# Scaling attention probabilities on GpSimd ahead of the transposes, in place of spread reciprocals behind the product with the values

## Chip, cores, metric

One core of a Trainium2 chip (trn2). The metric is the device time of one execution in microseconds (us), the median of several runs. The engines are TensorE (PE; its weight loads PEld), VectorE (DVE), ScalarE (ACT), GpSimd (POOL) and SyncE (SP). Each works through its own queue in order; they meet only at semaphores.

## The reference, cut to what matters

Two layers of a hybrid backbone over 512 latent tokens and 256 context tokens, width 1024, all in float32. Each layer is a SwiGLU block, a token mixing, and a second SwiGLU block. The change touches the softmax attention inside the mixing:

```
def attend(q, k, v, scale):
    s = jnp.einsum('bqhd,bkhd->bhqk', q, k).astype(jnp.float32) * scale
    p = jax.nn.softmax(s, axis=-1).astype(v.dtype)
    return jnp.einsum('bhqk,bkhd->bqhd', p, v)
...
ya_x = blocked_attention(qa_x, jnp.concatenate([ka_c, ka_x], axis=1), jnp.concatenate([va_c, va_x], axis=1), MLA_SCALE)
yb_x = neighborhood_attention(qb_x, kb_x, vb_x, kb_c, vb_c, na_rpb, rows)
ya_c = attend(qa_c, ka_c, va_c, MLA_SCALE)     # layer 0 only, as yb_c
```

Eight heads of latent attention (query and key width 96, value width 64) and four heads of neighbourhood attention (width 64, with a position bias on the latent keys). Latent queries see 512 latent and 256 context keys; context queries, which only layer 0 needs, see the 256 context keys.

## The kernel before

Every float32 product is made of three: an operand is split into a high part (a rounded copy, by ACT) and a low part (the difference, by DVE or GpSimd), and TensorE adds high x high, high x low and low x high.

In each layer the attention is one loop over **chunks**: 128 queries of one head against all their keys. A pair of heads has 12 chunks in layer 0 (per head four of latent queries with 768 keys, two of context queries with 256) and 8 in layer 1 (four per head). There are six such pairs, four latent and two neighbourhood: 72 and 48 chunks. Every engine runs through a list of steps s written out by hand, several chunks in flight:

- TensorE (`attention_pe`, from L1471), step s: the scores of chunk s into one of two PSUM pairs (L1487 to L1489, behind the exp of chunk s - 2); the transposes of chunk s - 2 from `prob` into the single PSUM buffer `pmid` (L1503, behind its exp and behind the low half of chunk s - 3); half of the products with V of the pair of chunks that began at s - 4 (L1522 to L1524). Ahead of the first half of a pair it waits for the reciprocals and makes, for each of the two chunks, a product of the reciprocals, broadcast, with the identity (L1515). This spreads 1/sum, which lies one per partition (query), over the free axis, where the queries are once the values have been multiplied in.
- DVE (`attention_dve`, from L1598), step s: for latent queries of neighbourhood heads the scores plus bias into `prob` (L1612, L1614); the negated maximum of chunk s (L1617); the reciprocal of the sum of chunk s - 1 (L1623); for even s the multiplication of the copied result of a finished pair, `y_f`, by the spread reciprocals (L1630, behind ACT's copy); the low half of the transposed chunk s - 2 (L1638, `pt_lo`).
- ACT (`attention_act`, from L1533), step s: the high half of chunk s - 2 from `pmid` (L1556, `pt_hi`), for even s the copy of a finished pair from PSUM to `y_f` (L1563), then exp of chunk s with the sum of its row (L1570), and at the first chunk of a head the high parts of the next head's q and k (L1531). `prob` has three slots, `pmid` one, `pt_hi` and `pt_lo` four.
- GpSimd (`attention_pool`, from L1578): at the first chunk of a head both low parts of the next head (L1586; ahead of the first neighbourhood pair those of V too, 1536 columns wide), and at step 7 of a pair of heads the low part of a finished block of y (L1595; three blocks in the fifth pair). Else it is idle in the loop.

`a_exp`, `a_rsum`, `a_ptl`, `a_pv`, `a_out`, `a_copied` are the semaphores of exp, reciprocal, low half, product with V, finished y, copied y.

Of the kernel before, what the change touches and what calls it, by code (L numbers as in the profile page):

```python
# [29 lines left out]
P = 128  # L30
# [135 lines left out]
def program(nc, x, c, ctx_in, c_ctx, w_mod, b_mod, w_gate, w_up, w_down, w_in, g_cq, w_q_up, g_ckv, w_kv_up,  # L166
            g_mla_q, g_mla_k, g_na_q, g_na_k, na_rpb, w_pool, pool_scale, w_out,
            k_ident, k_perm, k_cos, k_sin, k_invcnt, out, na_bias):
    with ExitStack() as ctx:
        def sem(name):  # L170
            return ctx.enter_context(nc.semaphore(name))
# [5 lines left out]
        def sb(name, shape, dt, at=None, off=0):  # L177
# [127 lines left out]
        a_hi, a_lo, v_hi_done = sem("a_hi"), sem("a_lo"), sem("v_hi_done")  # L305
        a_s, a_max, a_exp, a_rsum, a_copied, a_t, a_pth, a_ptl, a_pv, a_out, a_bias = (
            sem(f"a_{k}") for k in ("s", "max", "exp", "rsum", "copied", "t", "pth", "ptl", "pv", "out", "bias"))
        a_latent_t, a_latent_hi, a_latent_lo = (sem(f"a_latent_{k}") for k in ("t", "hi", "lo"))
# [1162 lines left out]
        def attention_pe(eng, l):  # L1471
# [4 lines left out]
            for s in range(n + 4):  # L1476
# [14 lines left out]
                if 2 <= s < n + 2:  # L1491
                    c = s - 2
                    keys = chunk_info(l, c)[4]
                    eng.wait_ge(a_exp, c0 + c + 1)
                    for part, (a, b) in enumerate(PARTS):
# [9 lines left out]
                if s >= 4:  # L1505
# [3 lines left out]
                    if part == 0:  # L1509
                        eng.wait_ge(a_ptl, c0 + 2 * b + 2)  # L1510
                        wait_if(eng, a_out, c0 // 2 + b - 1)
                        eng.wait_ge(a_rsum, c0 + 2 * b + 2)
                        for h in range(2):
                            at = (b % 2) * 512 + (2 + h) * P
                            eng.matmul(psum2[:, at:at + P], stat[:, (2 * b + h) % STATS, 2:3].broadcast_to([P, P]),  # L1515
                                       ident[:, :], start=True, stop=True)
                    vh, vl = (v_hi, v_lo) if kind == "mla" else (vn_hi, vn_lo)
# [15 lines left out]
        def attention_act(eng, l):  # L1533
# [8 lines left out]
            for s in range(n + 5):  # L1542
# [15 lines left out]
                if s >= 6 and s % 2 == 0:  # L1558
# [4 lines left out]
                    eng.activation(y_f[r, i if kind == "mla" else 4 + i, q0:q0 + 2 * P], psum2[r, bank:bank + 2 * P],  # L1563
                                   ACT.Copy).then_inc(a_copied, 1)
                if s < n:
# [12 lines left out]
        def attention_pool(eng, l):  # L1578

            n, w = n_chunks(l), y_cols(l)[-1][1]  # L1580

            def split(g):
                first, operands = splits(g)
                for m, (src, hi, lo) in enumerate(operands):
                    eng.wait_ge(a_hi, ATT_SPLITS * l + first + m + 1)
                    eng.tensor_tensor(lo, src, hi.bitcast(F32), ALU.subtract).then_inc(a_lo, 1)  # L1586

            split(0)
            for s in range(n):
                g, new = att_group(l, s)  # L1590
                if new and g + 1 < GROUPS:
                    split(g + 1)
                for k in y_split_at(l, s):
# [4 lines left out]
        def attention_dve(eng, l):  # L1598

            c0, n = ATT_C0[l], n_chunks(l)  # L1600
            for s in range(n + 5):
# [16 lines left out]
                if 1 <= s <= n:  # L1618
                    c = s - 1
                    eng.wait_ge(a_exp, c0 + c + 1)  # L1620
                    if c >= STATS:
                        eng.wait_ge(a_pv, c0 // 2 + (c - STATS) // 2 + 1)
                    eng.reciprocal(stat[:, c % STATS, 2:3], stat[:, c % STATS, 1:2]).then_inc(a_rsum, 1)  # L1623
                if s >= 6 and s % 2 == 0:
                    b = (s - 6) // 2
                    kind, i, j, q0, _ = chunk_info(l, 2 * b)
                    r, bank = slice(j * 64, j * 64 + 64), (b % 2) * 512
                    y = y_f[r, i if kind == "mla" else 4 + i, q0:q0 + 2 * P]
                    eng.wait_ge(a_copied, c0 // 2 + b + 1)
                    eng.tensor_tensor(y, y, psum2[r, bank + 2 * P:bank + 4 * P], ALU.mult).then_inc(a_out, 1)  # L1630
                if 2 <= s < n + 2:
# [256 lines left out]
```

## Time and profile before

| | us |
|---|---|
| median of 3 runs | 3387.88 (3383.86 to 3390.73) |
| the profiled execution | 3380.54 |
| its span | 3379.0 |
| TensorE busy | 3233.9 (96%), 18746 matmuls |
| DVE busy | 1709.8 (51%) |
| ACT busy | 928.8 (27%) |
| GpSimd busy | 212.5 (6%) |

The profile is one execution. Its page gives busy time by engine, the span in 40 slices, the chain that ended last and the costliest groups of instructions; the trace behind it can be asked for the busy time of a stretch, for who waited for whom, and for the instructions in order of time. Matmuls overlap in their records (a product starts before the one ahead has ended), so distances between starts say more than durations. A few matmul records are missing. The loops lie at about 1004 to 1218 us (layer 0) and 2786 to 2947 us (layer 1).

### The profile page before, as it was taken

Reading aid. Unit: us, or ns where it says so; the run is one execution under the profiler, and the core shown is the slowest. Engines: PE = TensorE matmul, PEld = TensorE weight load, DVE = VectorE, ACT = ScalarE, POOL = GpSimd, SP = SyncE. Lnnn points to the kernel's source line nnn. Section 1 sums busy time; section 2 is a strip of 40 time slices with the busy share of each in tenths; the row PEclk is TensorE's granted clock in tenths of the full one; section 3 lists DMA queues with packets and bytes.
Section 4 is the critical chain, followed back from the end, with each engine's and each line's share of the span. In section 5 each row is a group of like instructions: output and inputs, shape, how many; then the busy total and the mean of one; then the engine's idle time right before and its main releaser. Section 6 shows DMA issues by size and latency. Waiting matters only on the chain. (4 is left out here: it accounts for less than half of the span.)

```text
span 3379.0 us, 48465 instructions
## 1 busy us (share of the span) xinstructions
PE 3233.9 (96%) x18746; PEld 2818.9 (83%) x18746; DVE 1709.8 (51%) x2923; ACT 928.8 (27%) x1399; POOL 212.5 (6%) x181
## 2 busy tenths in 40 slices
PE   6999999989999998999999899999989999999999
PEld 6888888878888877888888788888878889878887
DVE  2665366354356755652664665263354257743333
ACT  1211122122136642211222221112222237633221
POOL 0500000030002200000000000000020003200000
PEclk7899999999999998999999899999999999999999
DMA  4633233221100012332332233242112100123333
GB/s 156 143 121 117 80 122 107 76 62 48 37 12 1 24 38 75 122 120 64 123 121 73 81 121 107 65 124 82 56 53 56 31 7 12 37 80 99 95 94 93
DMA packets 418467, 264.73 MB, mean 78 GB/s; under 512 B 21604, under 2 KB 409224, under 8 KB 418344
## 3 DMA queue, kind: packets, MB, share of 16 engines
q1 hardware_dynamic: 413512, 254.16, 25.4%
q0 software_dynamic: 2752, 4.66, 0.8%
q10 hardware_dynamic: 2080, 4.19, 0.4%
q8 instruction: 86, 1.41, 0.2%
q14 instruction: 37, 0.30, 0.0%
HBM read 257.15 MB, written 6.68 MB: 78 GB/s over the span
## 5 line engine op out<-in xcount | busy, mean ns | idle before, releaser
L361 PE MATMUL pair<-h_hi,w_hi 128*128 128x512 f32 x3136 | 1103.7, 352 | 47.4 <-DVE h_lo L477 21.5
L362 PE MATMUL pair<-h_lo,w_hi 128*128 128x512 f32 x3136 | 1030.3, 347 | 0.0
L365 PE MATMUL pair<-h_hi,w_lo 128*128 128x512 f32 x3136 | 869.0, 348 | 0.0
L361 PEld LDWEIGHTS pair<-h_hi,w_hi 128*128 128x128 f32 x3136 | 598.0, 191 | 190.3 <-issue 49.6
L362 PEld LDWEIGHTS pair<-h_lo,w_hi 128*128 128x128 f32 x3136 | 598.7, 191 | 77.4
L335 DVE TENSOR_TENSOR w_lo<-w_raw,w_hi 128x1024 fp32r<-128x1024 f32 (+2 forms) x310 | 399.6, 1290 | 459.2 <-ACT w_hi L328 450.8
L328 ACT ACTIVATE w_hi<-w_raw 128x1024 fp32r<-128x1024 f32 (+2 forms) x310 | 337.5, 1090 | 735.1 <-PE pair L365 691.3
L365 PEld LDWEIGHTS pair<-h_hi,w_lo 128*128 128x128 f32 x3136 | 504.8, 192 | 16.8
L361 PE MATMUL pair<-s_hi,w_hi 128*128 128x512 f32 x1232 | 426.6, 346 | 0.0
L362 PE MATMUL pair<-s_lo,w_hi 128*128 128x512 f32 x1232 | 400.5, 344 | 0.0
L600 DVE SCALAR_TENSOR_TENSOR mod_acc<-mod_raw,cs,mod_acc 128x256 f32<-128x256 f32 x896 | 365.1, 478 | 0.0
L365 PE MATMUL pair<-s_hi,w_lo 128*128 128x512 f32 x1232 | 339.5, 345 | 0.0
L745 DVE SCALAR_TENSOR_TENSOR xT<-pair,mv,xT 128x512 f32 (+3 forms) x136 | 81.8, 636 | 490.6 <-PE pair L365 490.1
L361 PEld LDWEIGHTS pair<-s_hi,w_hi 128*128 128x128 f32 x1232 | 231.3, 188 | 54.3
L362 PEld LDWEIGHTS pair<-s_lo,w_hi 128*128 128x128 f32 x1232 | 231.4, 188 | 30.0
L721 ACT ACTIVATE s_hi<-sf 128x768 f32 (+3 forms) x88 | 69.8, 793 | 634.6 <-DVE sf L768 634.6
L365 PEld LDWEIGHTS pair<-s_hi,w_lo 128*128 128x128 f32 x1232 | 196.2, 190 | 6.8
L718 ACT ACTIVATE sg<-pair 128x768 f32<-128x768 f32 (+1 forms) x88 | 66.8, 759 | 426.3 <-PE pair L365 426.3
L768 DVE TENSOR_TENSOR sf<-pair,sg 128x768 f32<-128x768 f32 (+1 forms) x88 | 78.4, 890 | 173.1 <-PE pair L365 173.0
L771 DVE TENSOR_TENSOR s_lo<-sf,s_hi 128x768 f32 (+3 forms) x88 | 78.5, 892 | 92.0 <-ACT s_hi L721 92.0
L1638 DVE TENSOR_TENSOR pt_lo<-pmid,pt_hi 128x512 fp32r<-128x512 f32 (+1 forms) x216 | 107.5, 534 | 24.5 <-ACT pt_hi L1556 23.1
L1556 ACT ACTIVATE pt_hi<-pmid 128x512 fp32r<-128x512 f32 (+1 forms) x216 | 92.6, 475 | 93.8 <-PE pmid L1503 93.6
(192 smaller groups left out, 3466.3 us busy)
## 6 DMA issues: line engine op xcount, KB each, us to landing
mod_raw<-in_w_mod SPq DMA_DIRECT2D x64, 1024.0 KB, 5.0
w_raw<-in_w_ffn_gate SPq DMA_DIRECT2D x88, 512.0 KB, 3.8
w_raw<-in_w_ffn_up SPq DMA_DIRECT2D x88, 512.0 KB, 3.8
w_raw<-in_w_ffn_down SPq DMA_DIRECT2D x64, 704.0 KB, 4.6
w_raw<-in_w_in SPq DMA_DIRECT2D x34, 512.0 KB, 3.9
w_raw<-in_w_out SPq DMA_DIRECT2D x12, 512.0 KB, 4.0
w_raw<-in_w_q_up SPq DMA_DIRECT2D x16, 288.0 KB, 2.9
mod_first<-in_w_mod ACTq DMA_DIRECT2D x2, 2048.0 KB, 12.6
```

The source lines that it names most:

```text
L328: eng.activation(w_hi[:, t.odd, 0:w], raw[:, t.odd, 0:w], ACT.Copy).then_inc(w_hi_done, 1)
L335: eng.tensor_tensor(w_lo[:, t.odd, 0:w], raw[:, t.odd, 0:w], w_hi[:, t.odd, 0:w].bitcast(F32), ALU.subtract).then_inc(w_lo_done, 1)
L361: eng.matmul(dst, wh, rh, start=first, stop=False)
L362: eng.matmul(dst, wh, rl, start=False, stop=False)
L365: last = eng.matmul(dst, wl, rh, start=False, stop=end)
L600: eng.scalar_tensor_tensor(mod_acc[:, j, :], mod_raw[:, k, :], cs[:, k, j:j + 1], mod_acc[:, j, :], ALU.mult, ALU.add).then_inc(mod_step, 1)
L721: eng.activation(s_hi[:, bass.ds(i, 1), 0:w].rearrange("p a t -> p (a t)"), sf[:, 0:w], ACT.Copy).then_inc(s_hi_done, 1)
L745: last = eng.scalar_tensor_tensor(xT[:, bass.ds(d, 1), a:b].rearrange("p a t -> p (a t)"), pair[o.odd][:, a:b], mv[:, 2, bass.ds(d, 1), p] ...
L768: eng.tensor_tensor(sf[:, 0:w], pair[(o + 1).odd][:, 0:w], sg[:, 0:w], ALU.mult).then_inc(acc_free[(o + 1).odd], 1)
L771: eng.tensor_tensor(s_lo[:, bass.ds(i, 1), 0:w].rearrange("p a t -> p (a t)"), sf[:, 0:w], s_hi[:, bass.ds(i, 1), 0:w].bitcast(F32).rearra ...
L1556: eng.activation(pt_hi[:, a // P:b // P, c % 4, :], pmid[:, a:b].rearrange("p (k q) -> p k q", q=P), ACT.Copy).then_inc(a_latent_hi if a = ...
L1638: eng.tensor_tensor(pt_lo[:, a // P:b // P, c % 4, :], pmid[:, a:b].rearrange("p (k q) -> p k q", q=P), pt_hi[:, a // P:b // P, c % 4, :]. ...
```

## The change

The reciprocals are applied earlier and by another engine. GpSimd waits for the reciprocal of chunk s and multiplies `prob` of that chunk in place by it, one value per partition. The transposes wait for this (`a_norm`) where they waited for exp. The spread reciprocals on TensorE (L1515) and the multiplication of `y_f` on DVE (L1630) go; ACT's copy is the finished y. GpSimd's low parts, which were made together at the first chunk of a head, are dealt out: one operand behind the multiplication of each of the first chunks.

```
@@ attention_pe
-                    eng.wait_ge(a_exp, c0 + c + 1)
+                    eng.wait_ge(a_norm, c0 + c + 1)
...
                         eng.wait_ge(a_ptl, c0 + 2 * b + 2)
                         wait_if(eng, a_out, c0 // 2 + b - 1)
-                        eng.wait_ge(a_rsum, c0 + 2 * b + 2)
-                        for h in range(2):
-                            at = (b % 2) * 512 + (2 + h) * P
-                            eng.matmul(psum2[:, at:at + P], stat[:, (2 * b + h) % STATS, 2:3].broadcast_to([P, P]),
-                                       ident[:, :], start=True, stop=True)
@@ attention_act
-                                   ACT.Copy).then_inc(a_copied, 1)
+                                   ACT.Copy).then_inc(a_out, 1)
@@ attention_pool
-            split(0)
+            for m in range(2):
+                split(0, m)
+            at = 0
             for s in range(n):
                 g, new = att_group(l, s)
-                if new and g + 1 < GROUPS:
-                    split(g + 1)
+                at = 0 if new else at + 1
+                a = chunk_info(l, s)[4][0][0]
+                eng.wait_ge(a_rsum, c0 + s + 1)
+                eng.tensor_scalar(prob[:, s % 3, a:TOK], prob[:, s % 3, a:TOK], stat[:, s % STATS, 2:3], None,
+                                  ALU.mult).then_inc(a_norm, 1)
+                if g + 1 < GROUPS and at < len(splits(g + 1)[1]):
+                    split(g + 1, at)
@@ attention_dve
                     if c >= STATS:
-                        eng.wait_ge(a_pv, c0 // 2 + (c - STATS) // 2 + 1)
+                        eng.wait_ge(a_norm, c0 + c - STATS + 1)
                     eng.reciprocal(stat[:, c % STATS, 2:3], stat[:, c % STATS, 1:2]).then_inc(a_rsum, 1)
-                if s >= 6 and s % 2 == 0:
-                    b = (s - 6) // 2
-                    kind, i, j, q0, _ = chunk_info(l, 2 * b)
-                    r, bank = slice(j * 64, j * 64 + 64), (b % 2) * 512
-                    y = y_f[r, i if kind == "mla" else 4 + i, q0:q0 + 2 * P]
-                    eng.wait_ge(a_copied, c0 // 2 + b + 1)
-                    eng.tensor_tensor(y, y, psum2[r, bank + 2 * P:bank + 4 * P], ALU.mult).then_inc(a_out, 1)
```

## Rows read from the trace of the kernel before

**Rows 1.** The page: span, and busy us (share) xinstructions by engine.
```profile
span 3379.0 us, 48465 instructions
...
PE 3233.9 (96%) x18746; PEld 2818.9 (83%) x18746; DVE 1709.8 (51%) x2923; ACT 928.8 (27%) x1399; POOL 212.5 (6%) x181
```

**Rows 2.** Stretches, both loops: length, busy by engine, granted clock, DMA share, GB/s.
```profile
1008.00:1218.00 210.00, 186.83 (x1335) 168.78 (x1333) 145.03 (x332) 138.28 (x325) 48.74 (x26) 0.98 0.05 15
2788.00:2948.00 160.00, 152.96 (x1100) 140.17 (x1099) 123.74 (x252) 113.59 (x244) 45.02 (x26) 0.99 0.06 19
```

**Rows 3.** TensorE's waits in the same two stretches: us, times, longest.
```profile
PE pmid L1503 <- DVE pt_lo L1638: 20.1, 32, 1.2
...
PE pmid L1503 <- DVE pt_lo L1638: 2.8, 4, 1.0
```

**Rows 4.** Timeline, latent attention of layer 1: start, length, engine, line [idle before].
```profile
2804.38 0.82 PE L1503 MATMUL pmid<-ident,prob 128*128 128x128 f32 x6
...
2805.41 0.36 PE L1522 MATMUL psum<-pt_hi,v_hi 128*128 128x256 f32 x1
...
2805.46 0.15 DVE L1623 RECIPROCAL stat<-stat 128x1 f32<-128x1 f32 x1
...
2807.61 0.82 PE L1503 MATMUL pmid<-ident,prob 128*128 128x128 f32 x6
2807.81 0.96 DVE L1617 TENSOR_REDUCE stat<-pair 128x1 f32<-128x768 f32 x1 [0.22 <-PE pair L1489]
2808.19 0.36 PE L1522 MATMUL psum<-pt_hi,v_hi 128*128 128x256 f32 x1
...
2813.82 0.96 DVE L1617 TENSOR_REDUCE stat<-pair 128x1 f32<-128x768 f32 x1 [0.23 <-PE pair L1489]
```

**Rows 5.** Timeline, DVE, layer 0: maximum at the start of two sixes.
```profile
1022.28 0.96 DVE L1617 TENSOR_REDUCE stat<-pair 128x1 f32<-128x768 f32 x1 [0.69 <-PE pair L1489]
...
1121.50 0.96 DVE L1617 TENSOR_REDUCE stat<-pair 128x1 f32<-128x768 f32 x1 [0.63 <-PE pair L1489]
```

**Rows 6.** Timeline, layer 0: three turns of the ring, the second with L1630.
```profile
1046.73 0.85 PE L1503 MATMUL pmid<-ident,prob 128*128 128x128 f32 x6 [0.65 <-DVE pt_lo L1638]
1048.93 0.84 PE L1503 MATMUL pmid<-ident,prob 128*128 128x128 f32 x6 [0.64 <-DVE pt_lo L1638]
1052.26 0.85 PE L1503 MATMUL pmid<-ident,prob 128*128 128x128 f32 x6 [0.60 <-DVE pt_lo L1638]
...
1050.96 0.42 DVE L1630 TENSOR_TENSOR y_f<-y_f,psum 64x256 f32<-64x256 f32 x1 [1.45 <-ACT y_f L1563]
1051.42 1.02 DVE L1638 TENSOR_TENSOR pt_lo<-pmid,pt_hi 128x512 fp32r<-128x512 f32 x2
```

**Rows 7.** One line of the code, GpSimd's copies: shortest/median/longest ns.
```profile
L1380 POOL COPY k_f<-kr_f x16: 816/822/1353, 864.8 to 2652.9; 32x768 f32<-32x768 f32 x16
```

**Rows 8.** Groups by shape, GpSimd: busy us, mean ns, idle before.
```profile
L1586 POOL TENSOR_TENSOR qs_lo<-na_f,qs_hi 128x768 fp32r<-128x768 f32 x4 | 7.4, 1845 | 36.8 <-ACT qs_hi L1531 36.8
...
L1586 POOL TENSOR_TENSOR vn_lo<-vn_f,vn_hi 128x1536 fp32r<-128x1536 f32 x2 | 7.0, 3486 | 0.0
L1595 POOL TENSOR_TENSOR h_lo<-y_f,h_hi 128x512 fp32r<-128x512 f32 x5 | 6.5, 1291 | 43.1 <-ACT h_hi L1464 43.1
```

**Rows 9.** Timeline, neighbourhood attention of layer 1: a pair of chunks; transposes and reciprocal.
```profile
2892.33 0.95 DVE L1617 TENSOR_REDUCE stat<-prob 128x1 f32<-128x768 f32 x1
...
2894.73 0.87 PE L1503 MATMUL pmid<-ident,prob 128*128 128x128 f32 x6
...
2896.76 0.15 DVE L1623 RECIPROCAL stat<-stat 128x1 f32<-128x1 f32 x1
...
2899.01 0.95 DVE L1617 TENSOR_REDUCE stat<-prob 128x1 f32<-128x768 f32 x1
```

**Rows 10.** Timeline, DVE, layer 0: first bias of two neighbourhood heads, three sixes apart.
```profile
1138.84 0.69 DVE L1612 TENSOR_TENSOR prob<-pair,na_tt 128x512 f32<-128x512 f32 x1 [0.81 <-PE pair L1489]
...
1195.58 0.69 DVE L1612 TENSOR_TENSOR prob<-pair,na_tt 128x512 f32<-128x512 f32 x1 [0.82 <-PE pair L1489]
```

More of the change, by code:

```diff
@@ L305, in program @@
         a_hi, a_lo, v_hi_done = sem("a_hi"), sem("a_lo"), sem("v_hi_done")
-        a_s, a_max, a_exp, a_rsum, a_copied, a_t, a_pth, a_ptl, a_pv, a_out, a_bias = (
-            sem(f"a_{k}") for k in ("s", "max", "exp", "rsum", "copied", "t", "pth", "ptl", "pv", "out", "bias"))
+        a_s, a_max, a_exp, a_rsum, a_norm, a_t, a_pth, a_ptl, a_pv, a_out, a_bias = (
+            sem(f"a_{k}") for k in ("s", "max", "exp", "rsum", "norm", "t", "pth", "ptl", "pv", "out", "bias"))
         a_latent_t, a_latent_hi, a_latent_lo = (sem(f"a_latent_{k}") for k in ("t", "hi", "lo"))
@@ L1578, in attention_pool, with split @@
         def attention_pool(eng, l):
-            n, w = n_chunks(l), y_cols(l)[-1][1]
-            def split(g):
+            c0, n, w = ATT_C0[l], n_chunks(l), y_cols(l)[-1][1]
+            def split(g, m):
                 first, operands = splits(g)
-                for m, (src, hi, lo) in enumerate(operands):
-                    eng.wait_ge(a_hi, ATT_SPLITS * l + first + m + 1)
-                    eng.tensor_tensor(lo, src, hi.bitcast(F32), ALU.subtract).then_inc(a_lo, 1)
-            split(0)
+                src, hi, lo = operands[m]
+                eng.wait_ge(a_hi, ATT_SPLITS * l + first + m + 1)
+                eng.tensor_tensor(lo, src, hi.bitcast(F32), ALU.subtract).then_inc(a_lo, 1)
+            for m in range(2):
+                split(0, m)
+            at = 0
             for s in range(n):
                 g, new = att_group(l, s)
-                if new and g + 1 < GROUPS:
-                    split(g + 1)
+                at = 0 if new else at + 1
[5 more added lines that the diff above has]
+                    split(g + 1, at)
                 for k in y_split_at(l, s):
```

## Prediction

> **What bounds the kernel now.** I began with the page: TensorE is busy for 96% of the span, so time goes where TensorE's work is shortened or where it waits [rows 1]. The change touches only the two attention loops, so the second view is the table of stretches: the loop of layer 0 takes 210 us with 186.8 us of TensorE, that of layer 1 160 us with 153.0, both at 0.98 to 0.99 of the full clock [rows 2]. Everything else is untouched, and what follows a loop starts when the loop ends. The third view, TensorE's waits, tells the loops apart: in layer 0 its transposes (L1503) wait 20.1 us in 32 pieces for the low halves of DVE (L1638), in layer 1 2.8 us [rows 3]. The fourth is the timeline.
>
> In layer 1's latent attention TensorE is the bound. Two chunks take 6.01 us, from maximum to maximum. From the transposes to the products with V it takes 1.03 us in the chunk with the spread reciprocals (L1515) and 0.58 us in the other [rows 4]: L1515 costs 0.45 us a pair. A chunk of 768 keys without it is (6.01 - 0.45)/2 = 2.78 us, of which I give 0.68 to the transposes and 1.05 each to scores and to values (both stream 2304 columns). A context chunk (256 keys) takes a third: 0.93.
>
> In layer 0 each head has four full chunks and two context chunks, a "six". TensorE's work on a six is 4 x 2.78 + 2 x 0.93 + 3 x 0.45 = 14.3 us, yet the six sixes from 1022.28 to 1121.50 take 16.54 us each [rows 5]. The rest is a ring through the single buffer pmid: transposes, high half on ACT, low half on DVE, next transposes. Undisturbed it turns in 2.20 us (1046.73 to 1048.93), but where the multiplication by the reciprocals (L1630) stands ahead of L1638 on DVE and waits for ACT's copy, in 3.33 (1048.93 to 1052.26) [rows 6].
>
> **What the change takes away.** L1515: 60 pairs x 0.45 = 27 us of TensorE, worth that only where TensorE doesn't wait for something else. L1630: 0.42 us of DVE per pair, and its wait ahead of L1638.
>
> **What it adds.** 120 GpSimd multiplications, 96 of 768 columns and 24 of 256,, and a place for them in the path: maximum, exp, reciprocal, GpSimd, transposes. The scaled chunk c is wanted at step c + 2. Its reciprocal stands on DVE behind the maximum of chunk c + 1. Call E(c) the end of the issue of the scores of chunk c. Then the reciprocal of c begins at E(c+1) + 1.08 (2804.38 to 2805.46) and lasts 0.15 [rows 4]; with 0.08 to reach GpSimd, a multiplication of length m and 0.05 to reach TensorE, the transposes of c can begin at E(c+1) + 1.36 + m. They are due at E(c+2), 2.78 later. So m up to 1.42 is hidden where GpSimd has nothing else to do; beyond it every us costs half a us a chunk, because the delay returns every second step.
>
> The price m is in no row. From below: GpSimd's one-input copy of 768 columns, 0.82 us [rows 7]; from above: its two-input subtraction of 768 columns, 1.84 us [rows 8]. The multiplication has one wide input and one value per partition, so it is nearest to the copy: I take 0.95 (0.35 for 256 columns), an estimate: 0.82 plus an allowance of about 0.13 for fetching the value. The Trainium skill, GPSIMD Engine Reference, section 4.1, speaks against putting elementwise work on GpSimd (about half VectorE's speed with two inputs) but calls one input roughly line-rate. The two kinds of row, 1.84 and 0.82, agree with it. By its section 3.1 (1.03 cycles an element at 1.2 GHz for a port-bound loop) the body would be an estimated 0.66 us, under my lower bound; the sum would be some 20 us better than mine.
>
> **What is queued on GpSimd.** It also makes the low halves of the next head's q and k: before, both at once; now each behind the multiplication of the first and second chunk. A multiplication plus a subtraction is 0.95 + 1.80 = 2.75 us a step (start to start), just inside 2.78: in layer 1 this is hidden for m = 0.95, and for nothing larger. Three things aren't hidden. (a) In layer 0 the steps of a six are shorter (E to E 2.33, 2.33, 2.08, 1.38, 2.08, 2.78), so the queue costs time. (b) The low half of V for the neighbourhood heads takes 3.49 us [rows 8]; it now starts behind the third chunk of the last latent head. (c) The low halves of y (1.84 us in layer 0, 1.29 in layer 1 [rows 8]) fall between two multiplications, three in a row once per layer.
>
> **The sum, m = 0.95.**
> Layer 1, latent (32 chunks, TensorE-bound): 16 x 0.45 = 7.2 gained. V's low half begins at E(31) + 2.25 and ends at E(31) + 5.7, where the scores of chunk 32 were due at E(31) + 1.73: 4.0 lost.
> Layer 1, neighbourhood (16 chunks): now 6.68 a pair, 3.34 a chunk. The bias is added on DVE first, so the reciprocal begins at E + 2.03 (2894.73 to 2896.76) [rows 9]; two steps take 2.03 + 0.15 + 0.08 + 0.95 + 0.05 + 2.78 = 6.04, or 3.02 a chunk: 16 x 0.32 = 5.1 gained. Three low halves of y in a row (3.9 us against a slack of 2.1): 1.8 lost. At the end the last ring turns without L1630 and L1515: 1.0 gained.
> Together 7.2 - 4.0 + 5.1 - 1.8 + 1.0 = 7.5 gained.
> Layer 0, latent (8 sixes): with the ring at 2.20 and no queue on GpSimd a six would be 14.04. With it: the first multiplication ends at E(1) + 2.26, q's half at + 4.10, the second multiplication at + 5.05, k's half at + 6.89, the third at + 7.84; its transposes begin at + 7.89, the fourth's a ring later (+ 10.1), and with 2.78 + 2.33 to the next E(1) the six is 15.2 us. With a low half of y it is 17.0, with V's too 19.3. Four sixes of 15.2 gain 1.34 each, 5.4; two of 17.0 lose 0.9; the last loses 2.0 (from 17.3); the first gains 0.5. Together 3.0.
> Layer 0, neighbourhood (4 sixes): the three from 1138.84 to 1195.58 take 18.9 each [rows 10]. By the same steps with the longer DVE part a six becomes 15.8, and 19.3 with three low halves of y: 7.7 gained over the four. The loop's end: 1.0. Together 3.0 + 7.7 + 1.0 = 11.7.
> All: 7.5 + 11.7 = 19.2 us gained. The profiled execution (3380.5, span 3379.0) would come to 3361.3; the median of the runs shown, 3387.9, lies 7.3 above it, so I name 3387.9 - 19.2 = 3368.7, rounded to 3369.
>
> **The rivals.**
> A, slower: the multiplication costs GpSimd what a two-input one does, 1.84 us [rows 8]. In layer 1 the transposes of the first two chunks of a head then begin at E(1) + 3.2 and + 6.8, the next two at + 10.4 and + 13.2; four chunks take 13.2 us, not 12.0, 9 us over eight heads; V and y cost 5 more, and the neighbourhood chunks at 3.5 instead of 3.34 another 5: 19 lost. In layer 0 a six goes from 16.5 to 17.7 and to 19.5 with y, 16 for the latent heads, and 9 for the rest: 25 lost. 44 lost in all, 3432. For it: every elementwise row of GpSimd in the loops has this price. Against: all of them have two wide inputs. Between 0.95 and 1.84 the sum moves by 63/0.89 = 71 us per us, so it decides from m = 1.22 us on.
> B, no change: m between 1.12 and 1.31 puts gain and loss within 7 us, 3388. The removed L1515 and L1630 are then paid back by the queue on GpSimd.
> C, a larger gain: m at the copy's 0.82 and the first scaled chunks catching up within a six. Then the 27 us of L1515 come nearly whole and some of layer 0's 20.1 us of waiting: about 35 gained, 3353. Against: the queue's arithmetic above.
>
> **How the numbers follow.** Forecast 0.48; C 0.08; B 0.19; A 0.25. The forecast's own range is 3354 to 3380. The range has to take in B and the near part of A (m up to about 1.5: 3369 + 71 x 0.55 = 3408): 3352 to 3410, about 0.8. A measurement of this kernel can tell some 0.2% (6.8 us) from no change. Faster by more: forecast and C, 0.56; within: B, 0.19; slower: A, 0.25.
>
> **What would show it.** GpSimd's multiplications at 0.95 us for 768 columns, and two chunks of layer 1's latent heads at 5.56 us instead of 6.01, confirm the first two steps. TensorE's waits for pmid in layer 0 should now name GpSimd's prob where they named DVE's pt_lo, mostly in the second and third chunk of a head. One wait of about 4 us should stand before the scores of layer 1's first neighbourhood chunk, ended by GpSimd. Layer 1's neighbourhood chunks should come every 3.0 us. If m is above 1.4 even the quiet chunks of layer 1 wait, and the forecast is wrong in sign; if the waits on GpSimd are missing although m is near 0.95, the queue was overpriced and C is nearer.

## Result, and the profile after

The changed kernel takes 3478.41 us (median of 4 runs, 3475.90 to 3479.58), the kernel before 3386.66 (4 runs). The ratio is 1.0277, 95% interval 1.0264 to 1.0289: slower by 92 us. I had named 3369, with a range of 3352 to 3410 and 0.56 on faster. The time is outside the range, and the sign is wrong. In the experiments below one of the four executions of removed ran at a granted clock of 0.53 and took 6371.53 us; its ratio and interval leave it out.

| | before | after |
|---|---|---|
| median, us | 3386.66 | 3478.41 |
| profiled execution, its span | 3380.54, 3379.0 | 3475.90, 3474.1 |
| loop of layer 0, first scores to first output product | 216.4 | 277.5 |
| the same in layer 1 | 162.8 | 201.2 |
| a six (four full and two context chunks) of a latent head, layer 0, no low half of y behind it | 16.2 to 16.8 | 20.3 to 21.0 |
| a six with a low half of y behind it | 16.2 and 16.5 | 23.3 |
| four chunks of a latent head, layer 1 | 12.1 | 14.4 |

The two loops hold all of it: 61.1 + 38.4 = 99.5 us, against 95.1 in the span; the rest of the kernel came to 4.4 us less in this pair of executions.

The page of the changed kernel, its first lines and two of its costliest groups (answering [rows 1]):

```profile
span 3474.1 us, 48043 instructions
...
PE 3248.8 (94%) x18506; PEld 2825.0 (81%) x18506; DVE 1690.5 (49%) x2863; ACT 926.7 (27%) x1399; POOL 443.9 (13%) x301
...
PEclk6899999999988889999999999999999999899999
...
L1591 POOL TENSOR_SCALAR prob<-prob,stat 128x768 f32<-128x768 f32 x96 | 211.1, 2202 | 80.9 <-DVE stat L1625 80.9
...
L1591 POOL TENSOR_SCALAR prob<-prob,stat 128x256 f32<-128x256 f32 x24 | 22.2, 923 | 67.8 <-DVE stat L1625 67.8
```

The disputed price stands in the last two lines. GpSimd's multiplication of 768 columns takes 2.20 us, not 0.95; that of 256 columns 0.92, not 0.35. This is more than the upper bound I had set, 1.84 us. The trace of the kernel before had dearer GpSimd rows of about this width, outside the loops: a two-tensor multiplication of 64x776 at 2.23 us (L1370) and an addition of 128x791 at 2.58 (L1361). The prediction left them out. TensorE has 240 matmuls fewer and is still busy for 15 us more. The line PEclk (granted clock in tenths of full speed, 40 slices) has four slices of 8 where layer 0's loop runs.

The stretches that hold the two loops now (columns as in [rows 2]: length, busy PE, PEld, DVE, ACT, POOL with their counts, granted clock, DMA share, GB/s):

```profile
1008.00:1281.00 273.00, 201.74 (x1188) 180.31 (x1188) 133.68 (x297) 139.48 (x329) 175.32 (x98) 0.83 0.04 11
...
2846.00:3044.00 198.00, 157.29 (x996) 138.34 (x996) 115.28 (x227) 113.75 (x245) 149.81 (x74) 0.91 0.05 15
```

GpSimd went from 48.7 to 175.3 us in the first and from 45.0 to 149.8 in the second. The granted clock fell from 0.98 to 0.83 and from 0.99 to 0.91.

TensorE's waits in the same two stretches (what and where, who ended it: us, times, longest), answering [rows 3]:

```profile
PE pmid L1503 <- POOL prob L1591: 67.0, 40, 5.7
...
PE pmid L1503 <- POOL prob L1591: 27.5, 32, 2.7
PE pair L1487 <- POOL vn_lo L1581: 5.4, 1, 5.4
```

Where layer 0's transposes waited 20.1 us for DVE's low halves, they wait 67.0 for GpSimd's scaled probabilities; in layer 1 it was 2.8 and is 27.5. The single wait of 5.4 us is the low half of V, the one I had put at 4.0.

The timeline of one latent head in layer 1 shows how a step now runs (start, length, engine, line, [idle before and who ended it]), answering [rows 4]:

```profile
2863.77 2.20 POOL L1591 TENSOR_SCALAR prob<-prob,stat 128x768 f32<-128x768 f32 x1 [1.39 <-DVE stat L1625]
...
2865.94 1.83 POOL L1581 TENSOR_TENSOR qs_lo<-q_f,qs_hi 96x768 fp32r<-96x768 f32 x1
...
2866.03 0.87 PE L1503 MATMUL pmid<-ident,prob 128*128 128x128 f32 x6 [0.59 <-POOL prob L1591]
...
2867.76 2.20 POOL L1591 TENSOR_SCALAR prob<-prob,stat 128x768 f32<-128x768 f32 x1
...
2869.93 1.84 POOL L1581 TENSOR_TENSOR ks_lo<-k_f,ks_hi 96x768 fp32r<-96x768 f32 x1
...
2870.01 0.87 PE L1503 MATMUL pmid<-ident,prob 128*128 128x128 f32 x6 [0.99 <-POOL prob L1591]
...
2871.74 2.20 POOL L1591 TENSOR_SCALAR prob<-prob,stat 128x768 f32<-128x768 f32 x1
...
2874.00 0.88 PE L1503 MATMUL pmid<-ident,prob 128*128 128x128 f32 x6 [0.86 <-POOL prob L1591]
...
2878.16 2.20 POOL L1591 TENSOR_SCALAR prob<-prob,stat 128x768 f32<-128x768 f32 x1 [1.65 <-DVE stat L1625]
```

From 2863.77 to 2871.74 GpSimd has no gap: 2.20 + 1.80 = 4.0 us a step, where TensorE wants 2.78. The transposes begin 0.05 to 0.07 us behind each multiplication. 14.39 us lie between the first line and the last, the same place one head on. That is the queue of the prediction, with the other price. Put 2.20 into its chain, with E(1) again the end of the issue of the scores of chunk 1, and the transposes begin at E(1) + 3.56, + 7.56, + 11.56 and + 14.34, so a head takes 14.35 us; measured 14.4.

Layer 0 has a second effect, which the sum had not at all. Two waits on GpSimd in a row (transposes, timeline), and then four stretches of 3 us around them:

```profile
1077.30 0.88 PE L1503 MATMUL pmid<-ident,prob 128*128 128x128 f32 x6 [1.70 <-POOL prob L1591]
...
1083.04 1.54 PE L1503 MATMUL pmid<-ident,prob 128*128 128x128 f32 x6 [4.15 <-POOL prob L1591]
```

```profile
1079.00:1082.00 3.00, 0.00 (x0) 0.00 (x0) 1.39 (x4) 1.09 (x3) 3.00 (x3) 1.00 0.01 3
1082.00:1085.00 3.00, 1.96 (x9) 1.97 (x10) 0.12 (x1) 0.75 (x2) 3.00 (x2) 0.51 0.00 0
1085.00:1088.00 3.00, 3.00 (x16) 3.00 (x15) 1.40 (x4) 0.83 (x4) 0.39 (x2) 0.50 0.00 0
1088.00:1091.00 3.00, 3.00 (x21) 2.87 (x20) 1.17 (x3) 1.32 (x4) 0.69 (x1) 0.85 0.00 0
```

TensorE waits 4.15 us for a multiplication that stands behind a low half of y. Then the granted clock is 0.50 (the lower level, 1.2 GHz) for some six microseconds of dense work: the six transposes take 1.54 us in place of 0.88. Sixes without y are touched too. In each of them the transposes wait about 1.1, 1.7 and 2.4 us for GpSimd in a row, and behind the third the transposes took 0.96 to 1.54 us; the sixes of 20.3 us ran at a mean clock of 0.92, those of 21.0 at 0.84. In the kernel before, the sixes ran at 1.00.

### The profile page after: what moved, and what is told of

Read it like the earlier page. It is cut to its first block and busy times, and to the rows that moved or that the text cites. A ratio compares the mean times of both kernels' runs of the same rounds, so it can differ in the third digit from the quotient of the medians.

```text
span 3474.1 us, 48043 instructions
## 1 busy us (share of the span) xinstructions
PE 3248.8 (94%) x18506; PEld 2825.0 (81%) x18506; DVE 1690.5 (49%) x2863; ACT 926.7 (27%) x1399; POOL 443.9 (13%) x301
## 3 DMA queue, kind: packets, MB, share of 16 engines
q1 hardware_dynamic: 413512, 254.16, 24.5%
## 5 line engine op out<-in xcount | busy, mean ns | idle before, releaser
L365 PEld LDWEIGHTS pair<-h_hi,w_lo 128*128 128x128 f32 x3136 | 502.6, 191 | 16.7
L1591 POOL TENSOR_SCALAR prob<-prob,stat 128x768 f32<-128x768 f32 (+1 forms) x120 | 233.2, 1946 | 148.7 <-DVE stat L1625 148.7
L1503 PE MATMUL pmid<-ident,prob 128*128 128x128 f32 x624 | 112.0, 321 | 96.6 <-POOL prob L1591 94.5
L1503 PEld LDWEIGHTS pmid<-ident,prob 128*128 128x128 f32 x624 | 81.8, 163 | 115.7 <-POOL prob L1591 112.4
## 6 DMA issues: line engine op xcount, KB each, us to landing
mod_first<-in_w_mod ACTq DMA_DIRECT2D x2, 2048.0 KB, 12.4
```

Source lines behind the costliest of these rows:

```text
L365: last = eng.matmul(dst, wl, rh, start=False, stop=end)
L1503: last = eng.transpose(pmid[:, k * P:(k + 1) * P], prob[:, c % 3, k * P:(k + 1) * P], ident[:, :])
L1591: eng.tensor_scalar(prob[:, s % 3, a:TOK], prob[:, s % 3, a:TOK], stat[:, s % STATS, 2:3], None, ALU.mult).then_inc(a_norm, 1)
```

## Experiments

Two theories stood after this, which may both be true in part. **P (price):** my chain is right and only m was wrong; a GpSimd multiplication of 0.9 us would give the forecast time. **C (clock and the rest):** there are costs that the chain lacks, so that even at 0.9 us the forecast isn't reached. A third question was why m is 2.20: the form of the instruction, its operand of one value per partition, or the place beside DVE. The length of a six is the distance between the first maxima of two heads, as in [rows 5]; four chunks of layer 1 likewise. A "plain" six has no low half of y or V behind it.

### m_256: the price brought down to 0.92 us

```
-                eng.tensor_scalar(prob[:, s % 3, a:TOK], prob[:, s % 3, a:TOK], stat[:, s % STATS, 2:3], None,
+                eng.tensor_scalar(prob[:, s % 3, SEQ:TOK], prob[:, s % 3, SEQ:TOK], stat[:, s % STATS, 2:3], None,
```

> The changed kernel, but GpSimd multiplies only the last 256 columns of each chunk (the 512 latent columns stay unscaled, so that part of the computation is left out). The trace of the changed kernel has 0.92 us for a multiplication of this width and 2.20 us for 768. Theory P (the price of the multiplication was the wrong term, the rest of the sum holds): at about 0.92 us the forecast's sum applies, some 19 us below the kernel before, 3364 to 3376. Rival Q (the added link and the low halves queued behind it cost by themselves, whatever the multiplication takes): no gain or a loss, 3385 or more.

Measured: 3386.10 us against 3384.65, ratio 1.0001 (0.9991 to 1.0011). The multiplications took 922 ns. Every second latent head of layer 1 took 11.13 us for its four chunks, 5.56 a pair, which is the forecast's figure; the heads between took 11.4. A plain six took 15.07 (forecast 15.2). But a six with a low half of y took 19.2 (forecast 17.0), the fifth pair's with three of them 22.9 (19.3), a plain neighbourhood six 17.65 (15.8). The whole time is the one expected by the rival, 3385 or more, and not P's 3364 to 3376. Place by place, P is right in the plain latent sixes and heads and misses 17 us (3386 against 3369) elsewhere. The price explains 92 of the 109 us between forecast and result, and not all.

### removed: only what the change takes away

The kernel before without L1512 to L1516 and without L1624 to L1630.

> The kernel before without the spread reciprocals on TensorE (L1515) and without the multiplication of y (L1630), nothing in their place, so the probabilities stay undivided: the removals alone, GpSimd as before. Theory P: the ring of layer 0 turns in 2.20 us throughout and a six takes about 14.0 us instead of 16.5, layer 1's latent pairs 5.56 us instead of 6.01; together 35 to 45 us gained, about 3345. If the removed products lay beside other work, less than 10 us.

Measured: 3346.53 against 3384.65, 0.9876 (0.9856 to 0.9896), 38 us less. A six took 14.05 us, where the chain with the ring at 2.20 says 14.04; four latent chunks of layer 1 took 11.13 and 11.4 in turn. The gain of taking these two things away was there, and as large as expected (35 to 45). In the neighbourhood heads of layer 1 a chunk came every 3.12 us, not 2.95 to 3.02. A plain neighbourhood six of layer 0 took 16.7, where the forecast had 15.8. The timeline of DVE alone, in layer 1, says why:

```profile
2866.23 0.95 DVE L1612 TENSOR_REDUCE stat<-prob 128x1 f32<-128x768 f32 x1
2867.10 0.15 DVE L1618 RECIPROCAL stat<-stat 128x1 f32<-128x1 f32 x1
2867.17 1.00 DVE L1626 TENSOR_TENSOR pt_lo<-pmid,pt_hi 128x512 fp32r<-128x512 f32 x2
2868.30 0.69 DVE L1607 TENSOR_TENSOR prob<-pair,na_tt 128x512 f32<-128x512 f32 x1
2868.91 0.41 DVE L1609 COPY prob<-pair 128x256 f32<-128x256 f32 x1
2869.36 0.95 DVE L1612 TENSOR_REDUCE stat<-prob 128x1 f32<-128x768 f32 x1
```

No idle time in brackets: from maximum to maximum (2866.23 to 2869.36) DVE works without a gap for 3.13 us. The bound is DVE, at 3.12 a chunk, and no order of GpSimd's work gets below it.

### norm_dve: the same multiplication on DVE

GpSimd's low halves stand together at the first chunk of a head again, as in the kernel before. The main lines of the edit:

```
-                eng.tensor_scalar(prob[...], ..., ALU.mult).then_inc(a_norm, 1)      # GpSimd, L1591
...
                     eng.reciprocal(stat[:, c % STATS, 2:3], stat[:, c % STATS, 1:2]).then_inc(a_rsum, 1)
+                    a = chunk_info(l, c)[4][0][0]
+                    eng.wait_ge(a_rsum, c0 + c + 1)
+                    eng.tensor_scalar(prob[:, c % 3, a:TOK], prob[:, c % 3, a:TOK], stat[:, c % STATS, 2:3], None,
+                                      ALU.mult).then_inc(a_norm, 1)
```

> The same scaling ahead of the transposes, but by DVE, right behind its reciprocal, and GpSimd's low halves at the first chunk of a head as before. No row shows this form on DVE; its other forms of 768 columns take 0.70 (memset) to 0.96 us (maximum), so 0.5 to 0.9 is likely. Theory P: TensorE's wait on GpSimd is gone; layer 1's latent heads stay at 5.56 us a pair, the neighbourhood heads, which DVE bounds, get slower by 0.2 to 0.4 us a chunk; within 12 us of the kernel before on either side, 3375 to 3400, and far below the changed kernel. Rival Q (scaling ahead of the transposes is what costs, on whichever engine): near the changed kernel, 3440 or more.

Measured: 3408.60 against 3384.65, 1.0071 (1.0054 to 1.0087), outside the expected 3375 to 3400. DVE's multiplication, all 120 of it (shortest/median/longest ns), then two of them beside GpSimd:

```profile
L1621 DVE TENSOR_SCALAR prob<-prob,stat x120: 352/620/3424, 1008.9 to 2965.5; 128x768 f32<-128x768 f32 x96, 128x256 f32<-128x256 f32 x24
```

```profile
2867.16 1.85 POOL L1581 TENSOR_TENSOR qs_lo<-q_f,qs_hi 96x768 fp32r<-96x768 f32 x1 [8.46 <-ACT qs_hi L1526]
...
2867.40 2.02 DVE L1621 TENSOR_SCALAR prob<-prob,stat 128x768 f32<-128x768 f32 x1
...
2871.32 0.62 DVE L1621 TENSOR_SCALAR prob<-prob,stat 128x768 f32<-128x768 f32 x1
```

Alone it takes 0.62 us, a third of GpSimd's 2.20. Where GpSimd is in a low half (2867.16 to 2869.01) the same instruction takes 2.02 and ends 0.41 after GpSimd's, as if it had stood for most of that time. On DVE the step is cheaper, but it is held up when it meets GpSimd, and the rest of DVE's queue with it. In layer 0's loop TensorE waits 26.8 us for DVE's low halves and 8.7 for its multiplication.

### forms: four forms in one kernel

The changed kernel, with another form in each of three pairs of heads per layer.

```
+                if pair_n == 1:
+                    eng.tensor_scalar(dst, dst, 0.5, None, ALU.mult).then_inc(a_norm, 1)
+                elif pair_n == 2:
+                    eng.tensor_tensor(dst, dst, stat[:, s % STATS, 2:3].broadcast_to([P, TOK - a]), ALU.mult).then_inc(a_norm, 1)
+                elif pair_n == 3:
+                    eng.tensor_copy(dst, dst).then_inc(a_norm, 1)
```

> The changed kernel with another form of GpSimd's instruction in three of the six pairs of heads: second pair a constant (0.5) in place of the value per partition, third pair a product of two tensors with the reciprocal broadcast along the row, fourth pair a copy in place (these pairs are not divided by their sum, except the third). For the price of 768 columns. If fetching the value per partition is what is dear: constant near the copy's 0.82 us. If the form itself is: constant 2.2 us too, copy 0.82, two tensors 1.84 or more. The pairs with the copy should take 5.56 us per two chunks, those with 1.84 us about 6.6 in layer 1.

Measured in one execution, GpSimd's groups by shape (busy us, mean ns, idle before):

```profile
L1599 POOL TENSOR_SCALAR prob<-prob,stat 128x768 f32<-128x768 f32 x48 | 105.7, 2206 | 67.7 <-DVE stat L1632 67.7
...
L1593 POOL TENSOR_SCALAR prob<-prob 128x768 f32<-128x768 f32 x16 | 34.0, 2127 | 7.0 <-DVE stat L1632 7.0
...
L1595 POOL TENSOR_TENSOR prob<-prob,stat 128x768 f32<-128x768 f32 x16 | 23.4, 1465 | 7.4 <-DVE stat L1632 7.4
...
L1597 POOL COPY prob<-prob 128x768 f32<-128x768 f32 x16 | 13.2, 827 | 15.6 <-DVE stat L1632 15.6
```

Same buffer, same columns, same place. The value per partition is not the reason: with a constant it is 2127 against 2206 ns. The place isn't either: a copy there takes 827, as in [rows 7]. It is the form: the tensor-with-scalar form is the dearest of the four on GpSimd, dearer than the subtraction of two full tensors (1845, [rows 8]), and the two-tensor form with the reciprocals spread by the access pattern does the same arithmetic in 1465. Why the form is so dear, no run shows. The whole took 3454.71 us. The first sixes of the pairs of layer 0 follow the form: 20.1 us with the constant, 16.6 with the spread reciprocals, 14.7 with the copy.

### low_dve: the full price, without the queue

The changed kernel; the low halves of q, k, V and y go from GpSimd to DVE, behind its own low half of the chunk. Only the multiplications stay on GpSimd.

> The changed kernel with the full multiplication on GpSimd (2.20 us for 768 columns) and nothing else there: all low halves, of q, k, V and y, are made by DVE. Tells the price of the link itself from that of the queue. By the chain, reciprocal at E + 1.08, plus 0.28, plus 2.20, every second step: 3.17 us a chunk in layer 1's latent heads, 12.7 us a head (changed kernel 14.4), a six about 16.5 (changed 20.3 to 23.3); in all 3400 to 3420, so still 15 to 35 us slower than before. If the queue of low halves were harmless: 3470 or more. If it were the whole cost: 3385 or less.

Measured: 3438.00 against 3384.10, 1.0154 (1.0137 to 1.0171). The expected range, 3400 to 3420, is missed. Taking the low halves off GpSimd gives back about 40 us (3478.4 - 3438.0) net of what DVE pays for them, and 54 are left with the link of 2.20 us and that work. Four chunks of layer 1 took 13.0 us (expected 12.7). The latent sixes took 17.5 to 20.4, mostly 18.7, well over the 16.5 expected. The granted clock goes with them: the six of 17.5 ran at 1.00, those of 18.6 to 19.0 at 0.91, that of 20.4 at 0.83. Even at 1.00 a six is 1.0 us over the chain; that part wasn't separated from DVE's longer list.

### m_256_y: low halves of y and V off GpSimd, m at 0.92

m_256, with the low halves of y and V on DVE, those of q and k left on GpSimd.

> m_256 again (GpSimd multiplies only the last 256 columns, the rest stays unscaled), but the low halves of y and of V, which queued on GpSimd between two multiplications, are made by DVE; those of q and k stay. In m_256 the plain sixes of layer 0 take 15.07 us (forecast 15.2) and the heads of layer 1 11.13, but the sixes with a low half of y 19.2 (forecast 17.0) and the head with that of V 18.9 us. Theory P with this correction: these all fall to the plain ones, 20 to 27 us gained on m_256, about 3362. If instead the scaling ahead of the transposes costs something spread over all chunks: less than 8 us gained.

Measured: 3379.06 against 3384.10, 0.9984 (0.9975 to 0.9994), 5 us less where 22 were expected, and 7 less than m_256. The four chunks with V's low half fell from 18.86 to 15.98 us, but the sixes with y stayed at 19.4. DVE and GpSimd met again:

```profile
1059.88 1.84 POOL L1581 TENSOR_TENSOR qs_lo<-q_f,qs_hi 96x768 fp32r<-96x768 f32 x1
...
1060.35 2.19 DVE L1649 TENSOR_TENSOR h_lo<-y_f,h_hi 128x768 fp32r<-128x768 f32 x1
```

DVE's subtraction of two SBUF tensors, 0.95 us where it is alone, takes 2.19 beside a GpSimd low half. The next maximum and reciprocal stand behind it on DVE, so GpSimd's next multiplication starts late, TensorE waits 2.22 us for it, and the six runs at a clock of 0.82, as in m_256. The wait moved from GpSimd's queue to DVE's and cost the same.

### m_256_fill: the same wait with the clock held up

m_256, with products of the identity with itself (their result is not used) written into a spare region of PSUM, ahead of the transposes that wait for a multiplication behind y.

```
+                    late = len(y_split_at(l, c - 1)) if c else 0
+                    if late and s < n:
+                        ...
+                        for h in range((12 if l == 0 else 6) * late):
+                            at = (b % 2) * 512 + 2 * P
+                            eng.matmul(psum2[:, at:at + P], ident[:, :], ident[:, :], start=True, stop=True)
```

> m_256 with idle products (identity x identity, 0.22 us each, 12 for each low half of y in layer 0, 6 in layer 1) put on TensorE ahead of the transposes that wait for GpSimd behind a low half of y. The wait stays as long; TensorE only doesn't stand still in it. In m_256 the granted clock falls to 0.50 for about 6 us behind such a wait of 2.87 us. Theory R (the fall of the clock is the part of those sixes that the forecast missed): the clock stays at 1.00 and the sixes with y fall from 19.2 to about 17.0 us, the forecast's value. Rival (the queue alone makes them 19.2): they stay at 19.2 or get longer.

Measured in the latent sixes with y: 16.85 us against 19.2 in m_256, and 17.0 in my prediction. First m_256, without the filling: one late group of transposes and the stretches from its wait on:

```profile
1067.27 1.54 PE L1503 MATMUL pmid<-ident,prob 128*128 128x128 f32 x6 [2.87 <-POOL prob L1591]
```

```profile
1065.00:1068.00 3.00, 0.73 (x4) 0.73 (x5) 0.90 (x4) 0.60 (x2) 3.00 (x3) 0.64 0.00 0
1068.00:1071.00 3.00, 3.00 (x16) 3.00 (x14) 1.02 (x2) 1.57 (x5) 0.12 (x1) 0.50 0.00 0
1071.00:1074.00 3.00, 3.00 (x19) 2.96 (x19) 1.52 (x4) 1.32 (x4) 0.92 (x1) 0.72 0.00 0
```

and with it:

```profile
1058.87 2.84 PE L1500 MATMUL psum<-ident 128*128 128x128 f32 x24
...
1061.91 0.88 PE L1510 MATMUL pmid<-ident,prob 128*128 128x128 f32 x6 [0.20 <-POOL prob L1598]
```

```profile
1059.00:1062.00 3.00, 2.80 (x26) 2.61 (x25) 1.42 (x4) 1.23 (x4) 3.00 (x4) 1.00 0.01 3
1062.00:1065.00 3.00, 3.00 (x26) 2.91 (x27) 1.45 (x4) 1.71 (x6) 0.91 (x2) 1.00 0.00 0
```

The same GpSimd queue, the same wait, filled with useless work: the clock stays at 1.00, the transposes take 0.88 instead of 1.54, and the six is 2.3 us shorter. This shows the clock term by itself, in this place. The whole kernel took 3390.24 (one execution), not less than m_256. The plain neighbourhood sixes went from 17.65 to 18.7 and 18.9, that with three low halves of y from 22.9 to 24.5, and in layer 1 the latent heads with y from 11.4 to 12.4: there the filling was longer than the wait it was to fill. So it shows the mechanism in the latent sixes and is no better kernel.

### shared: the two engines each scale a part

Two-tensor form on GpSimd for 512 columns, DVE's multiplication for the 256 context columns, of the latent heads. DVE also scales the chunks of context queries, which have only those columns, and makes y's and V's low halves; GpSimd scales the neighbourhood chunks of 768 columns alone.

> A complete kernel. The reciprocals still go ahead of the transposes, but as cheaply as the runs allow: for latent heads GpSimd multiplies the 512 latent columns, with the two-tensor form and the reciprocal broadcast (1.47 us for 768 columns and 0.61 for 256 in the run of forms, so about 1.04 for 512), DVE the 256 context columns (0.35 us) at the same time; neighbourhood chunks with 768 keys by GpSimd alone (1.47); the low halves of y and V on DVE. By the same chain: reciprocal at E + 1.08, 0.28, 1.04, so hidden in layer 1 (11.2 us a head), sixes about 15.3; 10 to 22 us faster than the kernel before, about 3368. If any link ahead of the transposes costs more than it gives back: 3385 or more.

Measured: 3415.76 against 3384.10, 1.0086 (1.0069 to 1.0103); expected about 3368. It was the furthest miss of the runs:

```profile
2862.59 1.23 DVE L1649 TENSOR_SCALAR prob<-prob,stat 128x256 f32<-128x256 f32 x1
...
2862.63 1.04 POOL L1608 TENSOR_TENSOR prob<-prob,stat 128x512 f32<-128x512 f32 x1 [0.26 <-DVE stat L1646]
```

Both wait for the same reciprocal, so in the latent chunks they start together, and DVE's part, 0.35 us alone, takes a median of 1.23: longer than GpSimd's own 1.04. The split didn't let the two parts run side by side. How much of the miss this explains wasn't separated: DVE also has the low halves of y and V here.

### tt_form: the change in its cheaper form

```
-                eng.tensor_scalar(prob[:, s % 3, a:TOK], prob[:, s % 3, a:TOK], stat[:, s % STATS, 2:3], None,
-                                  ALU.mult).then_inc(a_norm, 1)
+                eng.tensor_tensor(prob[:, s % 3, a:TOK], prob[:, s % 3, a:TOK],
+                                  stat[:, s % STATS, 2:3].broadcast_to([P, TOK - a]), ALU.mult).then_inc(a_norm, 1)
```

> The changed kernel with one thing different: GpSimd multiplies with the two-tensor form, the reciprocal broadcast along the row, which took 1.47 us for 768 columns and 0.61 for 256 in the run of forms (the changed kernel's form 2.20 and 0.92). A complete kernel. If the time follows the price m (m_256 3386 at 0.92, changed kernel 3478 at 2.20, 72 us per us): about 3425. If the price of 768 columns hardly matters beyond the link: near 3470.

Measured: 3416.42 against 3385.74, 1.009 (1.0075 to 1.0105); expected about 3425. One instruction's form, 2.20 to 1.465 us, is worth 62 us (3478.4 - 3416.4), two thirds of the loss. Latent heads of layer 1 come back to 12.1 us, as before the change. The chain says the same: a multiplication and a low half are 1.47 + 1.80 = 3.27 us a step, 0.49 over 2.78, twice in a head, on top of 11.13.

### all_dve: nothing on GpSimd in the loop

norm_dve, with the low halves on DVE as well.

> norm_dve (DVE multiplies) with the low halves of q, k, V and y made by DVE as well, so that GpSimd does nothing in the loops. In norm_dve DVE's multiplication of 768 columns took 0.62 us in the median and up to 3.42. If the long ones are DVE standing still while GpSimd reads and writes: here all take about 0.62 us, and DVE's two-input low halves of 768 columns 0.95; if they come from something else they stay. Total by DVE's load (0.88 + 0.13 + 0.62 + 0.95, and 1.9 for q and k once a head): about 3.1 us a chunk in layer 1, 3390 to 3410.

Measured in one execution:

```profile
L1621 DVE TENSOR_SCALAR prob<-prob,stat x120: 352/620/622, 1010.3 to 2982.7; 128x768 f32<-128x768 f32 x96, 128x256 f32<-128x256 f32 x24
```

The longest multiplication falls from 3424 to 622 ns when GpSimd is idle: the long ones in norm_dve were the meeting of the two engines, nothing else. The time, 3421.59, is above the expected 3390 to 3410. In layer 1 the latent heads are DVE's: it is busy for 59.8 of 62.0 us (2838 to 2900), at a clock of 1.00. In layer 0 this isn't so: over the sixes from 1041.7 to 1135.7, 18.8 us each, DVE is busy for 73.5 of 94.0 us, TensorE waits 13.6 us in ten pieces for DVE's low halves, and the granted clock is 0.82. So moving everything to DVE brings waits and a fallen clock too; no run says what each costs.

### y_last: from the other end

The kernel before, with L1624 to L1630 moved behind L1638 in DVE's list, and nothing else. The wait for ACT's copy then stands behind the low half that the ring needs.

> The kernel before with one thing moved: DVE's multiplication of y by the spread reciprocals (L1630) stands behind the low half of the transposed chunk (L1638) and no longer ahead of it. A complete kernel; nothing of the change is in it. In the run of removed both L1515 and L1630 were gone and a six took 14.05 us instead of 16.54. If the forecast's ring is right, of these 2.5 us 1.35 are L1515 (3 x 0.45) and the rest is L1630 standing in the way: a six of about 15.4 here, layer 1's latent heads unchanged at 12.1, in all 9 to 16 us faster than before, about 3372. If the move gains nothing: TensorE's queue, not the ring, bounds the sixes.

Measured: 3366.94 against 3385.74, 0.9949 (0.9934 to 0.9963): 19 us less than the kernel before (expected 9 to 16), 111 less than the changed one. Plain sixes took 15.2 us (expected 15.4). The transposes' waits in layer 0's loop (1008 to 1210), and the turn of the ring that follows the moved multiplication (here L1631 is the low half, L1640 the multiplication):

```profile
PE pmid L1503 <- DVE pt_lo L1631: 13.7, 14, 1.7
```

```profile
1045.80 0.42 DVE L1640 TENSOR_TENSOR y_f<-y_f,psum 64x256 f32<-64x256 f32 x1
...
1045.92 0.82 PE L1503 MATMUL pmid<-ident,prob 128*128 128x128 f32 x6
...
1048.14 0.85 PE L1503 MATMUL pmid<-ident,prob 128*128 128x128 f32 x6 [0.69 <-DVE pt_lo L1631]
```

The turn is 2.22 us (1045.92 to 1048.14), where with L1630 in front it was 3.33 [rows 6], and the 20.1 us of waiting in 32 pieces [rows 3] are 13.7 in 14. Half of what the removals alone bring (38 us) lay in this order alone, with nothing left out and no work added.

## Why the prediction was wrong, point by point

**The step that failed is the choice of m.** "The multiplication has one wide input and one value per partition, so it is nearest to the copy: I take 0.95 ..." It is 2.20. The bounds of 0.82 and 1.84 rested on the count of wide inputs, and forms shows that this is not what sets GpSimd's time: copy 827, two tensors 1465 with the second one spread, 1845 for two full ones, tensor with scalar 2206 or 2127 ns. The upper bound came from the nearest row of another form, and I took it for the end of the range without any row of this form. It wasn't even the dearest GpSimd row of that width in the trace: L1370, a two-tensor multiplication of 64x776, takes 2.23 us. The Trainium skill, GPSIMD Engine Reference, section 4.1, calls an operation with one input roughly line-rate on GpSimd; the copy agrees (827 ns), the tensor-with-scalar form doesn't (2206 ns), and the measurement decides.

**Its weight came out right, in part by luck.** I had 71 us per us of m. Three kernels that differ from each other almost only in m give it: m_256 at 0.92 us takes 3386, tt_form at 1.47 takes 3416, the change at 2.20 takes 3478. That is (3478 - 3386) / (2.20 - 0.92) = 72 us per us, though 56 below 1.47 and 84 above it. With 71 x 1.25 = 89 the prediction becomes 3458. But the measured slope contains a fall of the clock that my sum doesn't have: layer 0's loop runs at 0.93 in m_256, at 0.87 in tt_form and at 0.83 in the change. So the agreement of 71 and 72 doesn't confirm the sum by itself; the lengths of single heads and sixes do that better. Rival A had the right mechanism and place (queue on GpSimd, quiet chunks of layer 1 late too, the text's "above 1.4 ... wrong in sign") and only its price was too low.

**The rest, some 20 us, is at least three terms.** A rest of 17 us stands in m_256 too: 3386 where I had 3369.

First, the clock. I counted each wait at its length, and the time that TensorE then loses at the lower clock is missing from the sum altogether. In m_256 a wait of 2.87 us was followed by 0.50 and 0.72, in the change one of 4.15 us by 0.51, 0.50 and 0.85, over three microseconds each. m_256_fill shows 2.3 us a time, in the two latent sixes where I had 17.0 and m_256 measured 19.2. In the changed kernel the loop of layer 0 runs at 0.83 and TensorE is busy 201.7 us there where it was 186.8, with 16 us of work (36 x 0.45) taken away. How much of the 92 us would go if the clock stayed up wasn't measured in the changed kernel itself.

Second, the neighbourhood chunks. In layer 0 of m_256 the plain sixes are 1.85 us over my sum and the one with three low halves of y 3.6, more together than the two latent sixes with y (2.2 each). I let TensorE and the chain set them, 3.02 us a chunk; DVE sets them, 3.12 in removed, so the 5.1 us gained there would have been some 3.5 at best. In layer 0 a plain neighbourhood six is 15.8 in my sum, 16.7 in removed and 17.65 in m_256, the last two at a clock of 1.00.

Third, what lies between removed and m_256 in such a six, 0.95 us at full clock. TensorE waits there 2.4 us in three pieces for GpSimd's multiplications, so the link is not hidden as I had it. No run takes this part further.

A small slip beside these: for the four neighbourhood sixes I wrote 7.7 us gained. My own 18.9, 15.8 and 19.3 give 3 x 3.1 - 0.4 = 8.9.

**What held.** L1515 costs a little under half a us a pair: 0.45 in the sum; in removed 0.50 by the heads of 11.13 us ((12.12 - 11.13)/2) and 0.36 by those of 11.4. The ring of pmid at 2.20 makes a six 14.04 (14.05). The queue at m = 0.95 makes it 15.2 (15.07), at 2.20 a head of layer 1 14.35 (14.39). V's low half makes one wait, ended by GpSimd (3.8 in m_256, where I had 4.0 at m = 0.95; 5.4 in the change). The waits in layer 0 name GpSimd's prob in place of DVE's pt_lo. Even the gain of what is taken away was there: 38 us in removed. With m = 2.20 the chain gives 18.9 for a plain six of layer 0, and 20.3 to 21.0 were measured, at granted clocks of 0.92 and 0.84; the difference goes with the clock, but wasn't isolated in this place.

**The range.** It reached only to m = 1.5, the near part of A, and I held 1.84 for the far end. With a form that no row showed, the far end was not a bound but a guess, and a chance of 0.25 on slower was too little. The sign turned at m = 1.22 by my own sum, while GpSimd's rows of this width, other than the copy, lay between 1.5 and 2.6 us.

## What to carry to other kernels

Price an operation by a row of its own form on its own engine. If there is none, neither a row with fewer inputs nor one with more is a bound, and the forecast should say which sign it has at twice the dearest row. Work moved to an idle engine stands in that engine's queue, and GpSimd at work can hold DVE up: look first at what can be reordered on the engine that has it, as in y_last, where one line behind another brought 19 us. And where a wait of some microseconds arises in a loop of dense matmuls, look at the granted clock behind it and add what it takes (2.3 us a time in m_256).

## What the runs showed of the hardware

- **GpSimd's forms.** 768 float32 columns on 128 partitions: copy 827 ns, two tensors with the second spread from one column 1465, tensor with scalar 2127 (constant) and 2206 (value per partition). 256 columns: 922 ns for a value per partition, 612 for the spread form. So the count of wide inputs doesn't order them: the copy and the tensor with a constant read the same tensor and lie at the two ends. Nor is the form all: two-tensor lines outside the loops take 2226 (64x776) and 2576 ns (128x791), the subtraction in the loops 1845.
- **DVE and GpSimd.** DVE's tensor-with-scalar multiplication takes 620 ns alone and up to 3424 beside GpSimd's subtractions; its subtraction of two SBUF tensors 0.95 and 2.19 us; a part of 256 columns 0.35 and 1.23. Without work on GpSimd the longest was 622. The Trainium skill, SBUF — State Buffer, "Who interferes with whom", says that DVE in its two-port modes contends with GpSimd for a shared pair of ports and that the one that issues second is blocked until the first is done; with two SBUF inputs, it says, DVE contends with a GpSimd instruction that reads SBUF. The traces agree in the main: DVE's multiplication, 2.02 us, started 0.24 us behind a GpSimd low half and ended 0.41 us after it, where alone it takes 0.62. That ports are the reason no run here shows.
- **The clock.** In m_256 a wait of 2.87 us in otherwise dense work was followed by a granted clock of 0.50 and 0.72 in the next six us; in m_256_fill, with the wait filled by products of the identity, it stayed at 1.00. In the changed kernel the transposes behind a wait of 2.39 us took 1.54 us in place of 0.88 in one six, 0.96 in another.
